# Seven weight splits of the first attention moved to GpSimd, with parameter turns, score reads and output products put in another order

## The reference

```
h = x @ w_in
qa, ka, va, qb, kb, vb = split(h)
qa, ka = rope(qa), rope(ka)
oa = windowed softmax(qa ka^T / 8, with a sink) va      # heads 0..7
ob = neighbourhood softmax(qb kb^T / 8 + bias) vb       # heads 8..15
x = layer_norm(alpha * x + concat(oa, ob) @ w_out)
```

## Time and profile before

| | |
|---|---|
| median of 3 runs | 1734.54 us (1733.07 to 1734.54) |
| profiled execution | 1736.41 us, span of the records 1734.4 us |
| TensorE matmul busy | 1704.4 us, 98% |
| VectorE busy | 1176.2 us, 68% |
| ScalarE busy | 923.0 us, 53% |
| GpSimd busy | 295.2 us, 17% |

### The profile page before, as it was taken

One profiled execution on the slowest core, in us unless ns is written; L12 is line 12 of the kernel. 1 busy time (PEld: TensorE's weight loads), 2 busy tenths in 40 slices (PEclk: granted clock), 3 DMA queues, 4 the chain that ended last, 5 costly groups with the idle time before them and its releaser, 6 DMA issues.

```text
span 1734.4 us, 25155 instructions
## 1 busy us (share of the span) xinstructions
PE 1704.4 (98%) x9689; PEld 1460.5 (84%) x9689; DVE 1176.2 (68%) x1565; ACT 923.0 (53%) x1269; POOL 295.2 (17%) x162
## 2 busy tenths in 40 slices
PE   8999999999999999999999999999999999999999
PEld 7767888899897788878888978888888889878887
DVE  5777765778576776577666885666666667857665
ACT  4564444545584544465445666544554456664443
POOL 5002100576260040010000740000000006500000
PEclk9999999999999999999999999999999999999999
DMA  9335655555504575536554533655465555425652
GB/s 284 136 98 170 218 193 191 154 176 159 182 2 146 167 235 193 191 125 211 187 185 168 176 116 121 206 185 191 150 214 192 193 176 165 145 97 195 193 193 97
DMA packets 204268, 293.83 MB, mean 169 GB/s; under 512 B 6474, under 2 KB 169776, under 8 KB 204192
## 3 DMA queue, kind: packets, MB, share of 16 engines
q1 hardware_dynamic: 201072, 285.56, 50.4%
q0 software_dynamic: 2688, 6.47, 1.5%
q10 hardware_dynamic: 432, 0.75, 0.2%
HBM read 291.71 MB, written 1.05 MB: 169 GB/s over the span
## 4 chain that ended last, share of the span: by engine, by line
PE 89%; DVE 5%; ACT 4%; issue 1%; POOL 1%; DMA 0%; SPq 0%; ACTq 0%; DVEq 0%; POOLq 0%
PE acc L2084 30%; PE pg L2084 14%; PE pg L2158 13%; PE pg L2162 12%; PE pg L2161 6%; PE pg L2159 6%; PE acc L2582 1%; DVE w_lo L1378 1%; ACT w_hi L852 1%; PE pg L2569 1%; PE pg L2684 1%; PE pg L2204 1%; POOL w_lo L752 1%; ACT op L867 1%; DVE op L1416 1%
## 5 line engine op out<-in xcount | busy, mean ns | idle before, releaser
L1378 DVE TENSOR_TENSOR w_lo<-w_raw,w_hi 128x2048 fp32r<-128x2048 f32 x231 | 540.5, 2341 | 165.4 <-ACT w_hi L852 165.3
L852 ACT CAST w_hi<-w_raw 128x2048 fp32r<-128x2048 f32 x269 | 513.0, 1908 | 68.5 <-PE pg L2084 28.3
L2084 PE MATMUL acc<-w_hi,op 128*128 128x512 f32 x1600 | 517.6, 393 | 1.7 <-DVE op L2014 1.6
L2158 PE MATMUL pg<-op,w_hi 128*128 128x512 f32 x960 | 382.3, 398 | 7.1 <-DVE op L1408 1.9
L2162 PE MATMUL pg<-op,w_hi 128*128 128x512 f32 x960 | 379.7, 396 | 0.0
L2084 PEld LDWEIGHTS acc<-w_hi,op 128*128 128x128 f32 x1600 | 300.3, 188 | 67.2 <-issue 8.1
L2084 PE MATMUL acc<-w_lo,op 128*128 128x512 f32 x800 | 311.5, 389 | 0.0
L752 POOL TENSOR_TENSOR w_lo<-w_raw,w_hi 128x2048 fp32r<-128x2048 f32 x38 | 175.1, 4618 | 682.6 <-DVE w_lo L1378 630.3
L2161 PE MATMUL pg<-op,w_lo 128*128 128x256 f32 x960 | 267.6, 279 | 0.0
L2159 PE MATMUL pg<-op,w_lo 128*128 128x256 f32 x960 | 266.3, 277 | 0.0
L2084 PE MATMUL pg<-op,w_hi 128*128 128x256 f32 x1184 | 221.9, 286 | 3.1 <-DVE op L1416 1.2
(11 more groups left out here) (346 smaller groups left out, 1709.6 us busy)
## 6 DMA issues: line engine op xcount, KB each, us to landing
w_raw<-in_mlp_w SPq DMA_DIRECT2D x64, 1024.0 KB, 5.3
w_raw<-in_ffn_w_gate SPq DMA_DIRECT2D x44, 1024.0 KB, 5.3
w_raw<-in_ffn_w_up SPq DMA_DIRECT2D x44, 1024.0 KB, 5.3
w_raw<-in_ffn_w_down SPq DMA_DIRECT2D x44, 1024.0 KB, 4.8
w_raw<-in_ssm_w_in SPq DMA_DIRECT2D x24, 1024.0 KB, 5.4
w_raw<-in_w_in SPq DMA_DIRECT2D x20, 1024.0 KB, 5.0
w_raw<-in_attn_w_in SPq DMA_DIRECT2D x8, 1024.0 KB, 10.2
w_raw<-in_ssm_w_out SPq DMA_DIRECT2D x8, 1024.0 KB, 4.9
```

The costliest lines, as they stand in the source:

```text
L852: act.copy(w_hi[:, u % RING, :], w_raw[:, u % RING, :]).then_inc(hi_ready, 1)
L1378: dve.tensor_tensor(w_lo[:, s, :], w_raw[:, s, :], w_hi[:, s, :].bitcast(F32), ALU.subtract) \
L2084: ins = pe.matmul(psum, l, r, start=first and i == 0, stop=last and i == 2)
L2158: pe.matmul(bank, hi, joined, start=k == 0, stop=False)
```

## The change

Five things change in the first attention. GpSimd does the splits of units 6 to 12, seven in all, and its eight bias additions go behind and between the first two of them. The first four parameter blocks are turned in n = 6 in place of n = 5, the fifth in n = 7 in place of n = 6, and VectorE's copies move one n later too. VectorE reads the scores of both heads of a pair before it looks for their maxima. In the tail VectorE goes pair by pair, where it interleaved single heads. TensorE's products are dealt out differently between the heads, with two of unit 11 put before the last `value_pair`.

```
 def by_pool(u):
-    return U_SSM + 2 <= u < U_SSM + 17 or u == U_FFN[0] + 1 or ...
+    return U_ATT + 6 <= u < U_ATT_OUT + 4 or U_SSM + 2 <= u < U_SSM + 17 or ...
...
 # GpSimd
-            for h in range(BH):
-                pool.tensor_tensor(na_bias[:, h, :, :]..., na_rows(h), att_const("mask_na")..., ALU.add)
+            for n in range(2):
+                split(U_ATT + 6 + n)
+                for h in range(4 * n, 4 * n + 4):
+                    pool.tensor_tensor(na_bias[:, h, :, :]..., na_rows(h), att_const("mask_na")..., ALU.add)
+            for u in range(U_ATT + 8, U_ATT_OUT + 4):
+                split(u)
...
 # ScalarE: the cast of unit 11 goes into n == 8, before exp_head(8)
+                    if n == 8:
+                        split(U_ATT_OUT + 2)
...
 # ScalarE, tail
+            for h in range(AQ, AQ + BH, 2):
+                turned_head(h)
+                turned_head(h + 1)
+                if h + 2 < AQ + BH:
+                    exp_head(h + 2)
+                    exp_head(h + 3)
+                pair_hi(h // 2)
+                if h == AQ + 2:
+                    split(U_ATT_OUT + 3)
...
 # VectorE, n loop
-                if n in (6, 7):
+                if n in (7, 8):
...
+                    score_take(h)
+                    score_take(h + 1)
                     softmax_max(h)
                     softmax_max(h + 1)
...
 # VectorE, tail
+            for h in range(AQ, AQ + BH, 2):
+                more = h + 2 < AQ + BH
+                if more:
+                    score_take(h + 2)
+                    score_take(h + 3)
+                softmax_norm(h)
+                if more:
+                    softmax_max(h + 2)
+                softmax_norm(h + 1)
+                if more:
+                    softmax_max(h + 3)
+                if h > AQ:
+                    pair_lo(h // 2 - 1)
+            pair_lo((AQ + BH) // 2 - 1)
...
 # TensorE, tail
             sums(0, 1)
             score_pair(AQ + 2)
+            sums(1, 5)
+            prob_turn(AQ)
+            sums(5, 6)
+            prob_turn(AQ + 1)
+            sums(6, 7)
+            score_pair(AQ + 4)
+            value_pair(AQ)
+            sums(7, 9)
+            prob_turn(AQ + 2)
...
+            sums(15, 16)
+            prob_turn(AQ + 7)
+            second_half(2, 0, 2)
+            value_pair(AQ + 6)
+            second_half(2, 2, 8)
+            pe.wait_ge(ot_ready, 8)
+            output(U_ATT_OUT + 3, 14, False, True)
```

More of the change, by code:

```diff
@@ L173, in by_pool @@
 def by_pool(u):
-    return U_SSM + 2 <= u < U_SSM + 17 or u == U_FFN[0] + 1 or any(U_MIX[l] + 2 <= u < U_MIX_OUT[l] + OUT_UNITS - 1 for l in range(DEPTH))
+    return U_ATT + 6 <= u < U_ATT_OUT + 4 or U_SSM + 2 <= u < U_SSM + 17 or u == U_FFN[0] + 1 or any(U_MIX[l] + 2 <= u < U_MIX_OUT[l] + OUT_UNITS - 1 for l in range(DEPTH))
 N_SUMS = 4 + 3 * DEPTH
@@ L1618, in softmax_max @@
             def softmax_max(h):
-                score_take(h)
                 dve.wait_ge(score_taken, h + 1)
@@ L1662, in _ @@
                     dve.wait_ge(fixed_ready, 1)
-                if n in (6, 7):
-                    dve.wait_ge(par_turned, 4 if n == 6 else 5)
-                    for b in range(4) if n == 6 else (4,):
+                if n in (7, 8):
+                    dve.wait_ge(par_turned, 4 if n == 7 else 5)
+                    for b in range(4) if n == 7 else (4,):
                         dve.tensor_copy(pcol[:, b * P:b * P + ROW_BLOCKS[b]], par_block(b)[:, 0:ROW_BLOCKS[b]]) \
@@ L2461, in _ @@
                     score_pair(0)
-                if n == 5:
+                if n == 6:
                     pe.wait_ge(par_in, 16 * N_PAR)
                     par_turn(0, 4)
-                if n == 6:
+                if n == 7:
                     pe.wait_ge(par_ready, 4)
@@ L2488, in sums, with second_half @@
                         ins.then_inc(unit_done, 1)
+            def second_half(n, i0, i1):
+                u = U_ATT_OUT + n
+                if i0 == 0:
+                    take(u)
+                for i in range(i0, i1):
+                    if i % 4 == 0:
+                        pe.wait_ge(ot_ready, 4 + 2 * (n - 2) + i // 4 + 1)
+                    ins = output_part(u, 8 + 2 * n, i, False, False)
+                if i1 == 8:
+                    ins.then_inc(unit_done, 1)
             sums(0, 1)
             score_pair(AQ + 2)
[L2492 to L2506, removed]
+            sums(1, 5)
[7 more added lines that the diff above has]
+            prob_turn(AQ + 2)
+            sums(9, 10)
+            prob_turn(AQ + 3)
+            score_pair(AQ + 6)
+            value_pair(AQ + 2)
+            sums(10, 12)
+            prob_turn(AQ + 4)
+            sums(12, 13)
+            prob_turn(AQ + 5)
+            sums(13, 14)
+            value_pair(AQ + 4)
+            sums(14, 15)
+            prob_turn(AQ + 6)
+            sums(15, 16)
[5 more added lines that the diff above has]
+            output(U_ATT_OUT + 3, 14, False, True)
             warm(pg[:, 3, :], 4)
```

10 lines of the change are left out of this document (5 added, 5 removed).

## The result

The changed kernel takes 1747.04 us (median of 4 runs, 1746.79 to 1747.33) against 1734.54 (4 runs, 1733.07 to 1736.42): a ratio of 1.0072, 95% interval 1.0054 to 1.0089. It is slower by 0.7%. The forecast was 1733.6, with a range up to 1738.5 and a chance of 0.15 for slower.

A forecast was written before the change was run, and what follows sets the result against it. TensorE, busy 98% of the span, was taken to bound the kernel. The terms -5.8 - 0.2 + 1.5 + 3.6 sum to -0.9 us: 1733.6 off the median of 1734.54, range 1727 to 1738.5.

The forecast's parts named there:

- Parameter turns, -5.8: Fifth parameter turn: 3.2 us of TensorE idle time and 2.7 of lost clock go, 5.8 us net.
- Bias additions, -0.2: GpSimd's eight bias additions, moved away, no longer slow VectorE's split near 29.6 us: gain 0.2 us.
- Splits on GpSimd: Units 6 to 12: 4.64 us each against 2.29, latency covered; VectorE additions of two SBUF inputs wait for the split's end.
- They clear each other: Pairs 0 to 7: a GpSimd split ends at 11.5 us, the next pair's additions come from 13.4 on.
- Rope, +1.5: Rope of the keys near 41 us: additions wait for GpSimd's split, TensorE idles 0.7 to 1.8 us, taken as 1.5.
- the other branch: Rope of the keys: GpSimd's split starts first, the first addition waits until 45.65, TensorE idles 1.8 us.
- Heads 8 and 14: Tail: norm's addition waits for GpSimd's split, 2.3 us at head 8 and 1.8 at 14; TensorE idles 2.4 and 2.1.
- the tail's +3.6: Tail, heads 8 to 14: TensorE's idle time 6.6 us against 3.0 before, 3.6 worse.
- The port costs nothing here: Rival, chance 0.25: rope, head 8 and head 14 aren't held; sum -6.4 us, 1728.1.
- The clock falls at head 8: Rival, chance 0.10: idle time of 2.4 us at head 8 lowers TensorE's clock once, costing 2.7; sum +1.8, 1736.3.
- Head 13 is caught too: Rival, chance 0.12: head 13's norm addition waits for unit 12's split, TensorE idles some 6 us; sum +5.2, 1739.7.
- line 1632 never long: Sign of a wrong prediction, for the rival without holds: VectorE's line 1632 never above 0.2 us.

The follow-up runs named there:

- copies ahead of the split: Changed kernel with all splits back on VectorE, parameter copies issued ahead of that unit's split: 1731.0 us; the same copies edit in the kernel before: 1730.13 us.
- bias first: Changed kernel with GpSimd's eight bias additions ahead of its splits, as before the change: 1743.76 us.
- the best kernel: Kernel before with only the parameter copies moved ahead of that unit's weight split on VectorE: 1730.13 us, the study's fastest median.

## Why the prediction was wrong, point by point

*Parameter turns, -5.8.* The size was right and the place too: copies on time are worth 5.9 us by the profiles (copies ahead of the split), 4.6 and 5.5 by the medians of the two runs. In the changed kernel the wait of 3.2 us did go, because GpSimd had taken the split that stood ahead of the copies; with the later turn alone it stayed. But the term also booked 2.7 us of clock, and those didn't come: head 3's wait of 4.6 us stands at the same place, and the granted clock was 0.86 and 0.80 where 1.00 was forecast.

*Bias additions, -0.2.* VectorE's splits took 2.29 us each in the changed kernel, as forecast. What TensorE had of it is too small to read.

*Splits on GpSimd: the step that failed.* The prediction charged only VectorE's additions of two SBUF tensors, the one of norm and the one of the rope, and let all else run free beside a split: VectorE "finds their maxima (to 86.9)" while "GpSimd's split runs to 86.9", and the scalings stand in norm at their price without GpSimd. The ground was that one operation with a single input, a reciprocal, had run free. It doesn't hold for all of them. The negated maximum and the scaling have one tensor input, with source and result in SBUF, and both were held: a maximum took up to 3.94 us (0.23 alone), two scalings up to 4.85 (0.62 alone). The reciprocal (166 ns with and without GpSimd) and the reduction were never held. The Trainium skill has both halves of this: SBUF — State Buffer, "Who interferes with whom", says that one SBUF input is free of GpSimd only outside the two-port modes, and that `copy`, `cast` and `tensor_scalar` can enter them, `tensor_reduce` can't on this chip. The forecast left that condition out. The traces here agree for `tensor_scalar` and `tensor_reduce`, with float32 tiles down to 128x2; no copy or cast from SBUF to SBUF stands beside GpSimd in the traces of before and after. One hint was in the trace of before, where two scalings of 256 columns took 0.62 us together and one addition of that width 0.42.

*"They clear each other".* For pairs 0 to 7 the prediction checked the next pair's additions, 1.9 us behind a split's end. The addition that was held is the last of the same pair, just ahead of a split. The split waits for the cast that follows the pair's last exponential, so this addition has the 1.89 us of the cast (62.04 to 63.93) in hand. Two scalings of head 2 took 2.25 us in place of 0.62 beside bias additions, and head 3's addition came 0.09 us after the split of unit 8 had begun, so it was held for all of it. Taking the bias additions away (bias first) cleared it: the 4.6 us wait stood on small holds just ahead.

*Rope, +1.5.* VectorE was first by a hair: its first addition and GpSimd's split both start at 40.73, only the second was held, and TensorE waited 0.4 us. The term was 1.1 us too high here; in the run with the bias additions first the other branch came, at 3.0 us.

*Heads 8 and 14, and the tail's +3.6.* The additions of both, named as the ones held, took 0.14 us. What was held was the maximum of head 9 (3.88) and of head 15 (3.94), each a few operations ahead, with `pair_lo` of the pair before queued behind it. So what TensorE missed was the low part of an output, not a head's probabilities. At the reading of head 8's scores the changed kernel was 2.3 us late (90.81 against 88.49), where the forecast had it 4.4 early (84.0 against 88.4). From there to the layer norm it takes 8.1 us more than before (10.4 late at the end), where +3.6 was forecast. TensorE's idle time there is 7.2 us (2.9, 3.2, 0.8 and a last one of 0.3) against 3.0. The other 3.9 us fit its lower clock behind the waits (0.90, 0.93, 0.92 and 0.74, against 1.00 in the best kernel between 90 and 120 us), but no run took the clock's part by itself.

*The rivals.* "The port costs nothing here" (no hold at all) is refuted by the holds. "The clock falls at head 8" was right in kind: it fell, twice in the tail. "Head 13 is caught too" didn't occur, though it had the right size for a held operation. None of them had the one that decided it, a hold of an operation with a single input. What the prediction had named as a sign of being wrong, line 1632 never long, half came true: it was long once, at head 3, where it had been excluded.

## What to carry to other kernels

Before a long elementwise operation goes to GpSimd, list every VectorE operation that can fall into its time by where its operands are, not by how many it has. Here those with two inputs in SBUF, and a scaling or negated maximum from SBUF to SBUF, waited for the end of the running GpSimd instruction; reductions, reciprocals, what read PSUM, and a scaling that wrote PSUM didn't. A short operation pays the whole rest of the long one, so if the work must be there, cut it into pieces (one to four won 7.7 us here, one to sixteen 11.3), and all of it: the 1.2 us additions that stayed whole went on holding VectorE. And when a transfer or copy is late, look first at what stands ahead of it in its own queue: moving its consumer later moves the wait along, moving 0.83 us of copies ahead of a 2.29 us split removed it.

## What the runs showed that was not expected

- A VectorE operation on 128x2 elements took 4.45 us beside a GpSimd subtraction of 4.52 us, against 0.15 alone. The cost went by the length of the other engine's instruction: the mean of the 128x2 maximum is 894, 457 and 308 ns with the split in one, four and sixteen pieces, and 229 without it.
- VectorE was busy for only 68% of the span, and still 20 us of holds on it (10.6 on maxima, 4.4 on additions, 1.6 on scalings, 3.5 on the keys' rope) came with 12.5 us of time, 16.0 against the same order with the copies on time: the held operations, and those queued behind them, are links between TensorE's steps.
- Single bias additions of 1.2 us hold VectorE as well. It was such holds that brought VectorE into reach of the long one.
